# Moving one VectorE multiplication, one block of transposes and one conditioning product earlier in a two-block transformer kernel

## The reference, cut to what matters

```python
# second_block, each of 2 layers: a vector of 6 x 1024 values from ada_w (1024 x 6144)
mod = (silu_c @ ada_w[i] + ada_b[i])[:, None, :]
mod_c = silu_cc @ ada_w[i] + ada_b[i]

# neighbourhood_mixer (layer 2): 256 latent tokens = 4 rows of 64, 32 heads of 32, 256 context tokens
def row_block(args):
    q_r, r = args
    ...
    bias = rpb_f[:, dr_idx[None, :, None], dc_idx[:, None, :]]      # relative position, per head
    bias = jnp.where(col_in[:, None, :], bias, -jnp.inf)
    s_loc = jnp.einsum('bqhd,bikhd->bhqik', q_r, k_band).astype(jnp.float32) + bias
    s_ctx = jnp.einsum('bqhd,blhd->bhql', q_r, k_c).astype(jnp.float32)
    s = jnp.concatenate([s_loc.reshape(b, nh, GRID_W, band), s_ctx], axis=-1)
    prob = jax.nn.softmax(s, axis=-1).astype(v.dtype)
    return (jnp.einsum('bhqk,bkhd->bqhd', p_loc, v_band) + jnp.einsum('bhql,blhd->bqhd', p_ctx, v_c))
...
y_lat = o @ w_o
```

## Time and profile before

| | before |
|---|---|
| median of 3 runs | 2115.38 us (2114.42 to 2117.17) |
| the profiled execution | 2118.92 us, span 2116.9 us |
| PE busy | 2045.9 us (97%) |
| DVE busy | 1272.1 us (60%) |
| ACT busy | 876.3 us (41%) |
| POOL busy | 184.3 us (9%) |
| chain that ended last | PE 78%, DVE 13%, issue 3%, ACT 3%, DMA 1% |
| granted PE clock | 0.995 of full speed |
| neighbourhood attention's loop | 1788.40 to 1884.70 us |
| ends of the projections | 107.91 us (layer 1), 528.17 us (layer 2) |

### The profile page before, as it was taken

How to read it: one execution, slowest core, us unless ns; L and a number is a source line. 1 busy time by engine, 2 the same in 40 slices (tenths; PEclk the granted TensorE clock), 3 DMA queues, 4 the chain that set the end, 5 groups by cost and what they waited for, 6 DMA issues and landing times.

```text
span 2116.9 us, 31361 instructions
## 1 busy us (share of the span) xinstructions
PE 2045.9 (97%) x12185; PEld 1672.0 (79%) x12185; DVE 1272.1 (60%) x2047; ACT 876.3 (41%) x1459; POOL 184.3 (9%) x175
## 2 busy tenths in 40 slices
PE   8999999999999999999999999999999999789997
PEld 7776899887768998877777778788888787567996
DVE  5656677476567773744444378634445823766667
ACT  5533566354335654422222224323322433755452
POOL 2020200000200000000000004000000420302000
PEclk9999999999999999999999999999999999999999
DMA  8477665644876655322222222332333262535662
GB/s 247 160 268 250 183 178 178 193 126 159 281 256 198 175 183 165 128 79 80 64 95 59 100 60 80 100 100 85 93 99 99 80 146 86 76 93 158 187 187 85
DMA packets 327156, 297.45 MB, mean 141 GB/s; under 512 B 35030, under 2 KB 248354, under 8 KB 326928
## 3 DMA queue, kind: packets, MB, share of 16 engines
q1 hardware_dynamic: 322960, 283.22, 44.7%
q0 software_dynamic: 4096, 12.84, 1.8%
HBM read 294.97 MB, written 1.05 MB: 140 GB/s over the span
## 4 chain that ended last, share of the span: by engine, by line
PE 78%; DVE 13%; issue 3%; ACT 3%; DMA 1%; DVEq 0%; POOL 0%; SPq 0%; ACTq 0%; POOLq 0%
PE ps L431 22%; PE ps L433 21%; PE ps L432 21%; DVE w_lo L420 4%; PE ps L1931 2%; PE ps L499 2%; PE ps L790 1%; DVE npr L2509 1%; DVE hid L1551 1%; PE ps L696 1%; PE ps L2376 1%; PE ps L704 1%; DVE qkv L1222 1%; PE ps L706 1%; PE ps L1912 1%
## 5 line engine op out<-in xcount | busy, mean ns | idle before, releaser
L420 DVE TENSOR_TENSOR w_lo<-raw,w_hi 128x1024 fp32r<-128x1024 f32 x428 | 525.4, 1270 | 354.7 <-ACT w_hi L412 354.5
L412 ACT ACTIVATE w_hi<-raw 128x1024 fp32r<-128x1024 f32 x428 | 428.6, 1051 | 554.3 <-PE ps L431 468.1
L431 PE MATMUL ps<-zt_hi,w_hi 128*128 128x512 f32 (+1 forms) x816 | 276.6, 339 | 4.5 <-issue 1.4
L433 PE MATMUL ps<-zt_hi,w_lo 128*128 128x512 f32 (+1 forms) x816 | 274.9, 337 | 0.0
L432 PE MATMUL ps<-zt_lo,w_hi 128*128 128x512 f32 (+1 forms) x816 | 274.9, 337 | 0.0
L431 PE MATMUL ps<-xt_hi,w_hi 128*128 128x256 f32 x896 | 255.6, 285 | 12.3 <-DVE w_lo L420 10.9
L432 PE MATMUL ps<-xt_lo,w_hi 128*128 128x256 f32 x896 | 252.0, 281 | 0.0
L433 PE MATMUL ps<-xt_hi,w_lo 128*128 128x256 f32 x896 | 251.9, 281 | 0.0
L431 PEld LDWEIGHTS ps<-xt_hi,w_hi 128*128 128x128 f32 x896 | 169.6, 189 | 20.3 <-DVE w_lo L420 11.6
L431 PEld LDWEIGHTS ps<-zt_hi,w_hi 128*128 128x128 f32 x816 | 154.1, 189 | 24.9 <-issue 3.7
L432 PEld LDWEIGHTS ps<-xt_lo,w_hi 128*128 128x128 f32 x896 | 169.8, 189 | 0.0
(11 more groups left out here) (382 smaller groups left out, 3424.7 us busy)
## 6 DMA issues: line engine op xcount, KB each, us to landing
raw<-in_mlp_w SPq DMA_DIRECT2D x128, 512.0 KB, 4.6
raw<-in_ada_w SPq DMA_DIRECT2D x96, 512.0 KB, 5.2
raw<-in_w_up SPq DMA_DIRECT2D x88, 512.0 KB, 5.1
raw<-in_w_in SPq DMA_DIRECT2D x56, 512.0 KB, 4.9
raw<-in_ret_w_in SPq DMA_DIRECT2D x48, 512.0 KB, 4.5
raw<-in_w_down SPq DMA_DIRECT2D x44, 512.0 KB, 4.0
raw<-in_nat_w_in SPq DMA_DIRECT2D x24, 512.0 KB, 5.0
raw<-in_w_out SPq DMA_DIRECT2D x16, 512.0 KB, 7.3
```

The lines of the kernel that those rows point to most:

```text
L412: nc.scalar.activation(w_hi[:, t, w], raw[:, s, w], ACT.Copy).then_inc(on("w_hi"), act.gives("w_hi"))
L420: ins = nc.vector.tensor_tensor(w_lo[:, t, w], raw[:, s, w], w_hi[:, t, w].bitcast(F32), ALU.subtract)
L431: first = nc.tensor.matmul(out_ap, l_hi, r_hi, start=start, stop=False)
L433: return first, nc.tensor.matmul(out_ap, l_lo, r_hi, start=False, stop=stop)
```

## The change

Three edits. `pe_mixer` waits for `tok_out` behind the first conditioning unit instead of ahead of it. In `pe_nat`, `turned(0)` moves behind `scores(2)`, so turn 2 has the same order as all others. In `dve_nat`, the division moves from behind `biased(g, (2, 3))` to behind `biased(g, (0, 1))`, ahead of `take(g - 2, 1)`; `nt_end` stays where it was.

```diff
@@ pe_mixer
             release(pe)
-            pe.eng.wait_ge(on("tok_out"), pe.takes("tok_out", 2))
             assert sum(ADA_AT.get(step, 0) for step in ["begin", *mixer_steps()]) == ADA_UNITS
             pe_ada(pe, ADA_AT["begin"])
+            pe.eng.wait_ge(on("tok_out"), pe.takes("tok_out", 2))
@@ pe_nat
             for g in range(GROUPS + 3):
-                if g == 2:
-                    turned(0)
                 if g < GROUPS:
                     scores(g)
-                if 3 <= g < GROUPS + 2:
+                if 2 <= g < GROUPS + 2:
                     turned(g - 2)
@@ dve_nat
                 if g < GROUPS:
                     biased(g, (0, 1))
+                if g >= 4 and g % 2:
+                    r = nr[:, (g - 4) // 2 % 2, :]
+                    dve.eng.wait_ge(on("n_val"), dve.takes("n_val"))
+                    V.tensor_tensor(r, r, ps[7][:, SEQ:2 * SEQ], ALU.mult).then_inc(
+                        on("n_div"), dve.gives("n_div"))
                 if 2 <= g < GROUPS + 2:
                     take(g - 2, 1)
                 if g < GROUPS:
                     biased(g, (2, 3))
-                if g >= 4:
-                    f = (g - 4) // 2
-                    r = nr[:, f % 2, :]
-                    if g % 2:
-                        dve.eng.wait_ge(on("n_val"), dve.takes("n_val"))
-                        V.tensor_tensor(r, r, ps[7][:, SEQ:2 * SEQ], ALU.mult).then_inc(
-                            on("n_div"), dve.gives("n_div"))
-                    elif f:
-                        nt_end(f - 1)
+                if g >= 6 and g % 2 == 0:
+                    nt_end((g - 4) // 2 - 1)
```

## The result

The changed kernel takes 2102.01 us (median of 4 runs, 2100.54 to 2105.07); the kernel before, run beside it, 2116.28. The ratio is 0.9935 (95% interval 0.9923 to 0.9947), which is a gain of 13.8 us with 11 to 16 in the interval (the medians differ by 14.3). A second comparison gave 0.9925 (0.9913 to 0.9937). Forecast were 12.8 us and 2102.6. The profiled execution took 2102.31 (span 2100.3), where 2106.1 was forecast; that is 16.6 less than the profiled one of before, which lay 2.6 above its median.

The account below looks back on a forecast made before the run. PE, busy 97% of the span, was taken as the bound, so only its idle or late work could be won. 7.1 + 1.1 + 0.6 + 2.3 + 2.0 - 0.3 = 12.8 us off 2115.38 gave 2102.6, range 2100.0 to 2107.8.

Parts of the forecast that it names:

- division, turns 5 to 13: Attention's odd turns: the earlier division lets `values` follow the transposes at once, 1.42 us in each of five turns, 7.1.
- turns 15 to 17 and the end: Attention's last turns: the earlier division gains 1.1 us at turn 15 and 0.6 at turn 17.
- third scores: Attention's turn 2: scores start 2.27 us earlier and the transposes fall into VectorE's work on them, gain 2.3.
- conditioning unit: Mixers, end of the projections: the unit fits into TensorE's wait of 1.17 us, gain 1.0 per layer, 2.0.
- windows: Attention's bias windows: 14.29 us left for each window's transfers, cost between 0.1 and 1.5 us, taken as 0.3.
- pauses in turns 8, 10, 12: Attention: no gain forecast; turns 5 to 16 taken to repeat one pair, with the even turn at 4.40 us.
- The first rival: Attention: the bias windows bind at 15.31 us each, 4.7 us lost over six pairs, 2107.3 us; chance 0.17.
- The rule: Attention's bias windows: HBM reads slow to about 2 us under high load; pairs of 10.1 us, time near 2108.5.
- The step that failed: Attention, window 7: 1.0 us late, but for TensorE's 1.23 us pause in turn 12, which stays and leaves 0.2 spare.

Follow-up runs that it names:

- the next version: The changed kernel with VectorE's first copy of a turn put behind all four bias operations: 2101.84 us, ratio 0.9923 to the kernel before.
- before's second: The kernel before run once more, unchanged, for its trace: 2117.94 us in one run.
- conditioning alone: The kernel before with only the first conditioning unit moved ahead of the wait for `tok_out`: 2113.76 us, ratio 0.9981.
- before without windows: The kernel before without the transfers of bias windows 2 to 7: 2114.76 us, ratio 0.9985.
- before with twelve: The kernel before with twelve transfers a bias window instead of eight, same bytes: 2115.94 us, ratio 0.9992.
- division alone: The kernel before with only VectorE's division moved: 2106.81 us, ratio 0.9949.
- third scores alone: The kernel before with only the third scores put ahead of the first transposes: 2114.38 us, ratio 0.9985.
- The changed kernel with twelve transfers: The changed kernel with twelve transfers a bias window instead of eight, same bytes: 2106.79 us, ratio 0.9939 to the kernel before.
- copy and transfers moved: The changed kernel with VectorE's first copy behind all four bias operations and window transfers released one head at a time: 2098.84 us, run again 2099.30.
- the changed kernel without windows: The changed kernel without the transfers of bias windows 2 to 7: 2099.85 us, ratio 0.9910 to the kernel before.

## Why the prediction was right

The loop went from 96.20 to 83.79, 12.4 us where I had 10.8 (7.1 + 1.1 + 0.6 + 2.3 - 0.3), and the mixers gave their 2.0. That makes 14.4 of the 16.6 between the two profiles. Part of the other 2.2 can be the clock: from 1295 to 1305 and from 1670 to 1680 it was granted at 0.83 and 0.66 in the trace of before, and at 1.00 around both places in the changed kernel's.

| term | forecast | measured in the traces |
|---|---|---|
| division, turns 5 to 13 | 5 x 1.42 = 7.1 | 5 x 1.32 = 6.6 |
| turns 15 to 17 and the end | 1.1 + 0.6 | 1.8 (S(15) to the output product: 15.67, now 13.90) |
| third scores | 2.3 | 2.2 |
| conditioning unit | 2.0 | 2.0 |
| windows | -0.3 | -1.45 (turns 4, 12, 14: 0.30, 0.26, 0.89) |
| pauses in turns 8, 10, 12 | 0, "which stays" | 3.3 |

**The division.** The mechanism held as written: input ready, `values` behind the transposes, the fourth bias operation late next. The term was 0.10 too large per turn because of one wrong reading: I took 1.21 us from scores to VectorE as what holds where VectorE released the scores, and 1.31 where it did not. The changed kernel has 1811.92 to 1813.23, 1.31, though `nsm` released these scores. It is the even turns that have 1.31 and the odd ones that have 1.21, in either kernel. An even turn's first bias operation also waits for the window's semaphore, an odd one's doesn't; that this is the cause wasn't tried.

**The third scores and the mixers.** Both arrived as worked out, to 0.1.

**The windows.** The first rival was there, forecast with a chance of 0.17 and 4.7 us, and took 1.45 and 0.9 in the two traces. I had window 7 on time only thanks to the pause of 1.23 in turn 12. The pause went and window 7 made turn 14 longer by 0.89 (0.73 in the second trace), close to the 1.0 that this step named. Denser windows did not take longer: window 3 took 13.64 us from its first issue (1800.60) to the end of POOL's second pair, window 7 15.59 (from 1837.45), where before they took 13.60 and 15.31. The Trainium skill's page "DMA: Bandwidth & Descriptors", section "Latency and other measured facts", says that a read of HBM takes longer under high load. The rule would have cost 5.9. Here the load rose from 42 to 48% of the transfer engines' time, and the landing of a window's transfer stayed at a median of 5.7 us, so the trace doesn't show it at this load.

**The step that failed** is "a pause of PE of 1.23 in turn 12, ahead of it, which stays". It and two others went, and they are the 3.3 us that pay for the windows and the 0.5 of the division. The trace of before already showed them: I had written that turns 5 to 16 repeat one pair, but turns 8, 10 and 12 took 5.71, 4.90 and 5.82 where 4.40 was assumed. That the sum came out close is in part luck, since two errors of opposite sign met: 3.3 not forecast, and 1.15 too little for the windows plus 0.5 too much for the division. The median of 2102.01 for a forecast of 2102.6 flatters it: the traces give 14.4 us where the sum had 12.8, and the interval of the runs holds both.

## What to carry to other kernels

Look for the instruction whose semaphore holds the bound engine, and how much unrelated work stands ahead of it in its own engine's list: 0.33 us of VectorE work moved past 1.8 us of other work was worth 1.3 us in every second turn. Price it by the next thing that is late (here the fourth bias operation, 0.33 later) and not by the wait that goes (1.69). Then count what else was sized for the slower pace: transfers with a chain of 13.6 to 15.6 us had over 17 and now have 14.5 (4.83 + 4.39 + 4.83 + 0.45), and the next version, whose odd turns are 0.4 to 0.5 us faster, lost all of it there until they were released earlier.

## What the runs showed of the hardware

**The granted clock in the hole of turn 3.** With `turned(0)` ahead of the third scores, TensorE stands idle for 3.36 us before the fourth scores. In four of six traces with this hole (before's second, conditioning alone, before without windows, before with twelve) the granted clock fell, from 0.2 us ahead of its end to 1.5 us behind it; in the other two (before's first, division alone) it did not. In none of the eight traces in which the third scores stand ahead and the hole is 1.36 us or less did it fall there. The second trace of before, in stretches of 1.5 us (the numbers behind POOL are the granted clock, the transfer share and GB/s):

```profile
1801.00:1802.50 1.50, 0.47 (x4) 0.47 (x8) 1.50 (x6) 1.50 (x6) 0.38 (x1) 0.78 0.96 136
1802.50:1804.00 1.50, 1.50 (x8) 0.05 (x4) 0.16 (x2) 0.49 (x2) 1.30 (x2) 0.50 0.56 60
1804.00:1805.50 1.50, 1.50 (x12) 1.45 (x9) 1.31 (x4) 0.30 (x1) 0.00 (x0) 0.58 0.17 30
1805.50:1807.00 1.50, 1.50 (x30) 1.32 (x32) 1.25 (x4) 1.50 (x4) 1.42 (x2) 1.00 0.01 1
```

Its scores and transposes in that stretch, and those of the kernel before without windows:

```profile
1802.03 2.09 PE L2376 MATMUL ps<-nk,nq 32*128 32x512 f32 x8 [3.36 <-DVE nsm L2509]
1804.05 2.53 PE L2388 MATMUL ps<-cst,npr 128*128 128x128 f32 x16
```

```profile
1801.46 1.14 PE L2372 MATMUL ps<-nk,nq 32*128 32x512 f32 x8 [3.36 <-DVE nsm L2505]
1802.53 3.29 PE L2384 MATMUL ps<-cst,npr 128*128 128x128 f32 x16
```

At 0.50 of full speed, the 1.2 GHz level, the scores take 2.09 and not 1.14, the transposes up to 3.29 and not 2.06, and from S(2) to S(4) it is 1.3 to 1.4 us longer (here 5.35 + 4.86 for 4.39 + 4.50). The Trainium skill's page "TensorE: Matmul & The Clock Gate", section "HAM oscillation", says that a long enough wait throttles the array's clock, and that the work behind it starts slow. The traces agree in part: the same wait did it in four of six, and in the kernel before without windows the scores behind it still ran at full speed and only the transposes were slow. The third scores' move gains 2.2 us in every trace, and some 1.3 more in those executions where the clock would have fallen. That can be why its runs moved by 3.2 while its trace, compared with a trace of before whose clock held, shows 2.2; the interval of the runs (1.3 to 5.1) holds the 2.2 as well.

**Other places where it fell.** The changed kernel with twelve transfers, turn 14, where the late window 7 makes TensorE wait (granted clock 0.50 from 1857.06 to 1859.06):

```profile
1856.28 2.01 PE L2376 MATMUL ps<-nk,nq 32*128 32x512 f32 x8 [2.51 <-DVE nsm L2507]
1858.22 2.73 PE L2388 MATMUL ps<-cst,npr 128*128 128x128 f32 x16
```

It fell behind the pause of 2.71 us in the second trace with copy and transfers moved, too. And just behind the loop, where TensorE waits 1.86 us for the last low part in every kernel, it fell in five of the fourteen traces (the changed kernel without windows and with twelve transfers, and all three of the versions with VectorE's first copy moved). A wait of 2.2 us with this copy moved alone and a pause of 2.24 in the kernel before with twelve had no fall behind them. So the length of the last wait alone doesn't tell whether the clock falls. What else decides isn't shown.

**Pauses that belong to a kernel.** TensorE's pauses named issue stood in the same turns in both traces of a kernel that was traced twice and in three kernels of the same pace (before, third scores alone, conditioning alone). Edits that don't touch TensorE's program changed them: VectorE's division alone removed them, twelve transfers a window put them elsewhere. They were gone without the window transfers. They are worth as much here (3.3 us with the slowed turns around them) as the smaller edits, and a forecast from one trace can't tell whether they stay.
